# Moving the second group's first projections out of the first group's attention

## The reference

```python
h = rms_norm(x, norm1_gain) * (1 + scale1) + shift1      # adaLN from silu(c) @ w_ada
z = h @ w_in                                             # q k v | B C X | g_att g_conv
q = rms_norm(q, q_gain); k = rms_norm(k, k_gain)         # per head of 64 channels
y_att  = band_attention(q, k, v) @ w_o_att               # 8 heads, chunks of 64, 8 chunks back
y_conv = (B * conv3(C * X)) @ w_o_conv
x = x + gate1 * ((sigmoid(g_att) * y_att + sigmoid(g_conv) * y_conv) @ w_o)
h2 = rms_norm(x, norm2_gain) * (1 + scale2) + shift2
# PEER: product-key search, 8 heads x 16 experts of 16384 for every token
u, v = expert_u[idx], expert_v[idx]
x = x + gate2 * sum_k(softmax(top)[k] * gelu(u[k] . h2) * v[k])
```

## Time and profile before

| what | us |
|---|---|
| time, median of three | 2258.91 |
| time of the profiled execution | 2249.99 |
| its span | 2248.2 |
| PE busy (matmul) | 1878.1 (84%) |
| DVE busy | 1197.8 (53%) |
| ACT busy | 704.4 (31%) |
| POOL busy | 591.3 (26%) |
| group 0's attention with group 1's ticks | 128.7 to 230.2 |
| gathers beside group 1's ticks | 413.2 to 1206.0 |
| gathers alone | 1206.0 to 2248.2 |

### The profile page before, as it was taken

How to read it: one execution, slowest core, us unless ns; L and a number is a source line. 1 busy time by engine, 2 the same in 40 slices (tenths; PEclk the granted TensorE clock), 3 DMA queues, 4 the chain that set the end, 5 groups by cost and what they waited for, 6 DMA issues and landing times.

```text
span 2248.2 us, 19632 instructions
## 1 busy us (share of the span) xinstructions
PE 1878.1 (84%) x6152; PEld 813.3 (36%) x6152; DVE 1197.8 (53%) x3160; ACT 704.4 (31%) x2186; POOL 591.3 (26%) x584
## 2 busy tenths in 40 slices
PE   5999988699999999999996777776777776777776
PEld 2865977344444443434432221221221221221211
DVE  2334129555654433345565677676776664544544
ACT  3134112123763222232223333333333333333332
POOL 0000000222222222222212433343433443333332
PEclk9999999899989999999998999999999999999999
DMA  9346513588768888877856999999999999999997
GB/s 400 139 187 244 218 71 138 224 320 318 263 239 317 314 296 348 299 280 269 243 205 253 398 405 418 393 412 399 403 421 411 384 413 380 422 411 417 408 403 299
DMA packets 102313, 718.33 MB, mean 320 GB/s; under 512 B 13440, under 2 KB 13440, under 8 KB 15552
## 3 DMA queue, kind: packets, MB, share of 16 engines
q0 software_dynamic: 82944, 604.02, 68.9%
q1 hardware_dynamic: 18544, 110.69, 12.7%
q10 hardware_dynamic: 720, 2.36, 0.3%
HBM read 712.30 MB, written 4.73 MB: 319 GB/s over the span
## 4 chain that ended last, share of the span: by engine, by line
PE 45%; DMA 28%; DVE 15%; issue 6%; ACT 5%; POOL 1%; SPq 0%; DVEq 0%; POOLq 0%; ACTq 0%
DMA ring<-in_expert_uv_dram,uidx 27%; PE ps L778 18%; PE ps L521 7%; DVE ring L1413 6%; PE ps L640 6%; PE ps L661 3%; PE ps L646 3%; PE ps L517 1%; ACT wdiag L1026 1%; ACT wsel L1021 1%; PE ps L551 1%; PE ps L701 1%; DMA ring<-in_wpack_dram 1%; PE ps L493 1%; PE ps L584 1%
## 5 line engine op out<-in xcount | busy, mean ns | idle before, releaser
L778 PE MATMUL ps<-ring,wdiag 128*64 128x512 f32 x2304 | 1089.5, 625 | 269.9 <-ACT wdiag L1026 259.0
L396 POOL DMA_INDIRECT ring<-in_expert_uv_dram,uidx x576 | 590.0, 1024 | 1587.3 <-PE ps L778 1192.5
L1413 DVE CUSTOM_DVE_ANT_0 ring<-ring,mA 128x1024 f32<-128x1024 f32 x576 | 701.0, 1223 | 515.3 <-DMA ring<-in_expert_uv_dram,uidx 512.1
L778 PEld LDWEIGHTS ps<-ring,wdiag 128*64 128x64 f32 x2304 | 268.7, 140 | 1000.6 <-ACT wdiag L1026 584.1
L1019 ACT ACTIVATE gel<-act_in 128x1 f32<-128x1 f32 x576 | 116.6, 202 | 883.6 <-DVE act_in L1413 883.0
L1026 ACT ACTIVATE wdiag<-repeat,wsel 128x64 f32<-128x64 f32 x576 | 200.3, 348 | 18.8
L1021 ACT ACTIVATE wsel<-gel,gsel 128x1 f32<-128x1 f32 x576 | 169.6, 294 | 18.7
L521 PE MATMUL ps<-hB,ring 128*128 128x384 f32 x320 | 113.2, 497 | 0.0
L640 PE MATMUL ps<-hB,ring 128*128 128x384 f32 x256 | 91.1, 499 | 0.0
L701 PE MATMUL ps<-hB,ring 128*128 128x384 f32 x256 | 90.7, 497 | 0.0
L521 PEld LDWEIGHTS ps<-hB,ring 128*128 128x128 f32 x320 | 57.7, 190 | 52.1 <-issue 19.5
(11 more groups left out here) (223 smaller groups left out, 1441.1 us busy)
## 6 DMA issues: line engine op xcount, KB each, us to landing
ring<-in_wpack_dram SPq DMA_DIRECT2D x96, 1024.0 KB, 7.1
ring<-in_expert_uv_dram,uidx POOLq DMA_INDIRECT x576, 8.0
xB<-in_x_b_dram SPq DMA_DIRECT2D x2, 1536.0 KB, 18.4
o_y_p<-mA ACTq DMA_DIRECT2D x8, 256.0 KB, 5.5
bias<-in_bias_dram SPq DMA_DIRECT2D x1, 1024.0 KB, 27.4
o_v_p<-kv SPq DMA_DIRECT2D x4, 256.0 KB, 9.2
o_k_p<-xB SPq DMA_DIRECT2D x4, 256.0 KB, 7.8
xB<-in_keysT_dram SPq DMA_DIRECT2D x1, 1024.0 KB, 9.3
```

The source lines that it names most:

```text
L396: nc.gpsimd.indirect_dma_start(out=row[:, n % NROW, :], out_offset=None, in_=ins["expert_uv"], in_offset=bass.IndirectOffsetOnAxis(ap=uidx ...
L778: mm = nc.tensor.matmul(pY[c * GT:(c + 1) * GT, half, :], wdiag[:, n % NDIAG, :], row[:, n % NROW, D + half * 512:D + (half + 1) * 512], s ...
L1413: nc.vector.tensor_tensor_reduce(r, r, h2n[:, g % 2, :], 1.0, 0.0, ALU.mult, ALU.add, act_in[:, g % 2, j:j + 1]).then_inc(s["dot"], 1)
```

## The change

One constant. `WITH_A` goes from 24 to 2:

```diff
-WITH_A = 2 + 2 * (8 + len(TOKENS[1]))
+WITH_A = 2
```

## The result

The changed kernel takes 2287.61 us (median of 4 runs, 2281.99 to 2301.4) against 2256.97 (4 runs, 2254.35 to 2259.63): a ratio of 1.0145, interval 1.0096 to 1.0193. A second, longer measurement of the same kernel gave 2282.36 against 2257.97, a ratio of 1.0113 (1.008 to 1.0146). It is slower by 31 us in the first measurement and by 24 in the longer one; the forecast was +12, 2271 us, with 2256 to 2292 as its range.

The account below looks back on a forecast made before the run. PE was taken to bound group 0's attention and the gathers beside ticks, fetching the gathers alone. -60 + 60 + 12 - 2.3 + 2 = +11.7 us on the 2258.9 median gave 2271 us, range 2256 to 2292.

Parts of the forecast that it names:

- Group 0's attention, -60: Group 0's attention loses the moved q, k, v and head-sum work; PE stays the pace: 101.5 to about 40 us.
- The work that comes in, +60: Gathers beside group 1's ticks: the moved pieces cost PE the same there, not hidden by fetching: +60 us.
- The new wait, +12: Folds beside q and k results wait for diagonals behind ACT's square root and gelu table load: seven of 1.3-1.4 us, one 2.3.
- The start, -2.3: Start of the gathers: more pieces ahead of fold 0 shrink PE's 2.78 us wait for the first diagonal: -2.3 us.
- Fewer folds beside group 1's attention: Group 1's attention ticks get 28.5 gathers, before 32.4; 3.9 folds move to other ticks, 2 us not won back: +2.
- Time held at nothing: Start, merge and search of group 0, and the gathers alone, keep their instructions and were given no change in time.
- the gathers alone stay at 1042 within 3: Last stage, bound by fetching with no instruction touched: claimed to stay at 1042 us within 3.
- No wait (1): Gathers beside ticks: PE reaches folds late anyway or attention also drops its idle; 2261 us, chance 0.14.
- The clock of group 1's attention (2): Group 1's attention leaves the half clock, granted clock about 0.98; faster, -9 us, 2250; chance 0.08.
- rival 3: Group 0's attention saves only 50 us, and the q and k stretch gets a 0.90 clock: +31, 2290; chance 0.12.
- The drain (4): Switch to gelu on ACT: the skill page's drain lengthens eight fold waits by 1.38 us: +10, 2281; chance 0.05.

Follow-up runs that it names:

- half_before: Kernel before, with a token tile's first half of gathers folded into output partitions 0 to 63, the second into 64 to 127: 2274.47 us, ratio 1.0062.
- pairs_before: Kernel before, with PE folding two gathers at every second gather up to gather 191: 2181.74 us, ratio 0.9657.

## Why the prediction was right, and what it missed

**Group 0's attention, -60: right.** 101.5 to 40.7 us. PE holds the pace, 2.24 us for a head (ada tick at 154.90, the next at 157.14), as worked out, and the weights came in time at a DMA share of 0.99:

```profile
154.90 1.06 PE L476 MATMUL ps<-ring,siluc 128*32 128x512 f32 x8
155.90 0.43 PE L551 MATMUL ps<-kc,mA 64*64 64x128 f32 x2
...
157.14 1.07 PE L476 MATMUL ps<-ring,siluc 128*32 128x512 f32 x8
```

**The work that comes in, +60: right.** L521 went from 68.3 to 114.8 us, L517 from 12.9 to 23.9, and L528 is new with 6.5: 64.0 us of records, some 62 as they overlap a little where they meet.

**The new wait, +12: right in mechanism and size.** 13.0 us in eight waits, one for each result; six of 1.37 or 1.38 and two longer ones, where I had seven and one. Ahead of the seventh (447.74) stands a v piece already, 1.99 us in place of 2.85, and PE comes that much earlier. Taking the waits out gave back 16.8 us of the stage and 10.9 of the median.

**The start, -2.3: right**, 2.78 to 0.59.

**"Fewer folds beside group 1's attention", +2: the term that was mis-sized.** It said that 3.9 folds of 1.86 us move to other ticks, "where PE pays in full". I had the counts, 183 and 161 ticks for 180 gathers, and asked only what they do beside the attention. That 161 ticks leave 19 gathers without one, so that two folds meet, and 183 leave none, I did not ask; every fold had the price 1.86 us, which was the price of a lone one. The folds became 16.7 us dearer (half_before against before shows the cause, pairs_before its size when all folds meet). Part came back: the idle of PE in the stretch of the last ticks fell from 10.4 to 3.7 us. The two long waits of before there, 3.30 and 5.04 us, each stand one tick behind a pair of folds (1099.54 and 1146.31), and the changed kernel has neither; half_before shows for one of them that pair and wait trade against each other. So the term measured some +10 (16.7 less 6.7) where I had 2. The sum of the stage is 62 + 13.0 - 2.2 + 16.7 - 6.7 = 83, measured 79 to 81.

The Trainium skill bears on it, and I could have weighed it: "TensorEngine Tiling (Array Packing)", section "Key Properties", says that different tiles of the array can load weights and multiply in parallel. These rows agree: 1.94 us for eight records in different halves, 3.65 in the same.

**Time held at nothing.** The merge grew by 2.2 us: its first 32 records take 7.36 us in place of 5.37, the granted clock 0.50 at their start, behind waits of 0.78, 0.46 and 0.68 us at the attention's end. The statement that the gathers alone stay at 1042 within 3 was wrong: the stage takes 1042 to 1070 us in executions of either kernel, and no number from one profile could hold it to 3. It was no part of the sum.

**The rivals.** No wait (1) falls by the eight waits. The clock of group 1's attention (2) was 0.94 where it had to reach 0.98, and in before it is 0.89 in one execution and 0.93 in the other. Of rival 3, the attention at 50 us falls with 40.7, the clock of 0.90 in the q and k stretch with a measured 1.00 (368 to 458); its +31 came near the 30.6 between the first medians for reasons that were not its own. The drain (4) falls by 378.57 to 378.58: the rule in "ScalarE: Activation LUTs" of the Trainium skill holds here for the load's 1.28 us alone.

So 2271 was 11 to 17 us low, and the rise 24 to 31 us where 12 was forecast. That 2256 to 2292 held the time was luck as far as the folds go: the room above came from rival 3, whose mechanism did not occur.

## What to carry to other kernels

When work is spread over a schedule, count what stands next to what, before and after: a record's price in a trace is its price beside these neighbours, and a smaller busy sum for the same number of records, with a mean that is no shorter, tells that some lay side by side. Folds that write different halves of the output partitions belong next to each other in the queue, with both their diagonals ready; here that is worth 78 us alone and 108 with this change (2147 us), and it decided the change's sign. A table load between two others costs only if something waits for what stands behind it, so let the engine finish what is due first.

## What the hardware showed that was not expected

- Two neighbouring folds into output partitions 0 to 63 and 64 to 127 take 1.94 us together, one takes 1.93; into the same half two take 3.65. The pair costs 1.94 only if the second fold's diagonal is there in time: nine of the 19 pairs of before took 2.77 to 6.31.
- The same gathers, the same instructions: 1042, 1050, 1056 and 1070 us in four profiled executions, at 397, 394, 391 and 386 GB/s. The cause is open.
